# The recurrence's level product with X over both heads of a pair: 128 rows, with Z as two blocks on a diagonal, and M V in one buffer

## What is computed

```python
def step(S, inp):
    r_t, w_t, k_t, v_t, a_t, b_t = inp
    sa = jnp.einsum('bhij,bhj->bhi', S, a_t)
    S = S * w_t[:, :, None, :] + sa[..., None] * b_t[:, :, None, :] + v_t[..., None] * k_t[:, :, None, :]
    return S, jnp.einsum('bhij,bhj->bhi', S, r_t)
```

## Time and profile before

| | |
|---|---|
| median of three runs | 1658.82 us |
| the profiled execution's own time | 1659.36 us |
| its span, first to last instruction | 1657.6 us |
| TensorE busy with products / loading weights | 1457.2 us (88%) / 890.2 us (54%) |
| VectorE, ScalarE, GpSimd busy | 635.0, 365.4, 205.5 us |
| the recurrence within the span | 453.6 to 650.9 us: 197.3 us |

### The profile page before, as it was taken

One profiled execution on the slowest core, in us unless ns is written; L12 is line 12 of the kernel. 1 busy time (PEld: TensorE's weight loads), 2 busy tenths in 40 slices (PEclk: granted clock), 3 DMA queues, 4 the chain that ended last, 5 costly groups with the idle time before them and its releaser, 6 DMA issues. The chain is left out here.

```text
span 1657.6 us, 27544 instructions
## 1 busy us (share of the span) xinstructions
PE 1457.2 (88%) x10747; PEld 890.2 (54%) x10748; DVE 635.0 (38%) x1062; ACT 365.4 (22%) x788; POOL 205.5 (12%) x263
## 2 busy tenths in 40 slices
PE   6999999957778898999929999994996599999968
PEld 4566666645578886444414444442795344444423
DVE  1122453079245452776461111114795311111127
ACT  1233110066423332111101111111232011111111
POOL 4000000000133322110001101104000110110040
PEclk9999999987789999999959999996697699999989
DMA  6573110041110002110259788785105778786453
GB/s 189 134 290 121 26 26 26 0 113 27 30 26 4 5 4 71 56 39 26 111 169 314 267 303 289 254 282 181 62 1 186 269 246 314 257 281 227 159 209 124
DMA packets 137060, 236.96 MB, mean 143 GB/s; under 512 B 20178, under 2 KB 100115, under 8 KB 136682
## 3 DMA queue, kind: packets, MB, share of 16 engines
q1 hardware_dynamic: 113458, 151.01, 28.7%
q0 software_dynamic: 16880, 60.41, 9.9%
q10 hardware_dynamic: 6624, 24.12, 3.6%
HBM read 178.84 MB, written 58.21 MB: 143 GB/s over the span
## 5 line engine op out<-in xcount | busy, mean ns | idle before, releaser
L2257 PE MATMUL ex_pb<-ew_w_gate_up,ex_xT 128*128 x736 | 329.8, 601 | 6.0 <-DVE ex_xT L2302 2.3
L298 PE MATMUL pj_pb<-pj_xT,pj_w 128*128 128x348 f32 (+3 forms) x960 | 282.1, 455 | 0.8 <-ACT pj_xT L322 0.8
L298 PEld LDWEIGHTS pj_pb<-pj_xT,pj_w 128*128 128x128 f32 (+1 forms) x960 | 178.8, 186 | 101.9 <-ACT pj_xT L322 0.8
L2257 PEld LDWEIGHTS ex_pb<-ew_w_gate_up,ex_xT 128*128 128x128 f32 x736 | 138.0, 193 | 165.0 <-issue 164.0
L2240 PE MATMUL ex_pb<-ew_w_down,ex_hiddenT 128*128 x368 | 165.7, 593 | 3.4 <-ACT ex_hiddenT L2327 3.4
L2450 DVE TENSOR_TENSOR ex_hidden<-ex_hidden,ex_pb 128x256 f32<-128x256 f32 x46 | 19.4, 421 | 324.4 <-ACT ex_hidden L2322 324.4
L2240 PEld LDWEIGHTS ex_pb<-ew_w_down,ex_hiddenT 128*128 128x128 f32 x368 | 66.3, 190 | 69.9 <-issue 69.9
L2445 DVE COPY ex_y_rows<-ex_pb 128x512 f32<-128x512 f32 x46 | 31.8, 692 | 134.5 <-PE ex_pb L2240 134.5
L430 DVE SCALAR_TENSOR_TENSOR mixed<-pj_pb,v_mu,mixed 128x347 f32<-128x347 f32 (+3 forms) x42 | 24.0, 572 | 145.7 <-ACT mixed L372 145.6
L2322 ACT ACTIVATE ex_hidden<-ex_pb 128x256 f32<-128x256 f32 x46 | 17.7, 384 | 261.3 <-PE ex_pb L2257 261.3
L1888 PE MATMUL mo_pb<-late_rows,projected_qkv 128*128 128x512 f32 (+1 forms) x144 | 66.6, 608 | 0.0
(11 more groups left out here) (414 smaller groups left out, 2031.4 us busy)
## 6 DMA issues: line engine op xcount, KB each, us to landing
ew_w_gate_up<-in_w_ex_gate SPq DMA_DIRECT2D x32, 1024.0 KB, 8.2
ew_w_gate_up<-in_w_ex_up SPq DMA_DIRECT2D x32, 1024.0 KB, 10.9
ew_w_down<-in_w_ex_down SPq DMA_DIRECT2D x32, 1024.0 KB, 12.9
scratch_slots_out<-ex_y_rows ACTq DMA_DIRECT2D x46, 512.0 KB, 4.8
scratch_slots_out<-pj_tmp POOLq DMA_DIRECT2D x4, 4096.0 KB, 16.7
scratch_x_stored<-x_rows SPq DMA_DIRECT2D x16, 512.0 KB
pj_w<-in_w_in SPq DMA_DIRECT2D x7, 1024.0 KB, 8.9
minus_kk_then_y<-in_x_prompt SPq DMA_DIRECT2D x8, 512.0 KB, 6.0
```

The lines of the kernel that those rows point to most:

```text
L298: last = nc.tensor.matmul(product(at)[:, 0:tn], w[:, s % NW, k, c0:c0 + mrows], xT[:, k, x0:x0 + tn], start=(k == 0), stop=(k == KD - 1))
L2257: last = mm(pb[:, 2 + u, :], xT[:, u, k, :], w[:, k, :], start=(k == 0), stop=(k == KD - 1))
```

## The change

In `level_x` the two products of a pair's heads become one over all 128 rows. X of both heads is read as it lies; Z is kept as a 128x64 matrix with the first head's 64x32 block at the upper left, the second's at the lower right and zeros elsewhere. The zeros come from the mask: the level constants grow from 64x32 (stacked twice) to 128x64 with two blocks on the diagonal, and `take_z` writes each column of Z twice, under the two halves of the mask, 128x512 elements in place of 128x256. The product goes to columns 256 to 511 of bank 6 in place of banks 6 and 7, and `take_x` on VectorE adds both heads in one instruction of 128x256. `MV` becomes one buffer; ScalarE's copy into it waits until both chunks of the step before have been added (`asc`).

```diff
-        Z = m.sb("Z", [P, 2, 4, HALF])
+        Z = m.sb("Z", [P, 2, 4, 2, HALF])
-        MV = m.sb("MV", [P, 2, DA])
+        MV = m.sb("MV", [P, DA])
@@ take_mv
                 act.wait_ge(q["mv"], n + 1)
-                nc.scalar.copy(MV[:, n % 2, :], pb[:, 3, :]).then_inc(q["mvc"], 1)
+                if n:
+                    act.wait_ge(q["asc"], 2 * n)
+                nc.scalar.copy(MV[:, :], pb[:, 3, :]).then_inc(q["mvc"], 1)
@@ level_x
                 for t in range(4):
-                    for par in range(2):
-                        for ch in range(2):
-                            last = mm(pb[fr(ch), 6 + par, P * t:P * t + HALF], X[fr(par), ch, t, :], Z[fr(par), ch, t, :],
-                                      start=True, stop=True)
+                    for ch in range(2):
+                        last = mm(pb[fr(ch), 6, 256 + CH * t:256 + CH * t + CH], X[:, ch, t, :],
+                                  Z[:, ch, t, :, :].rearrange("p a b -> p (a b)"), start=True, stop=True)
@@ take_z
-                tt(flat(Z[:, :, :, :]), columns(6, 0, HALF), eight(f"lev{lev + 1}T"), ALU.mult).then_inc(q["zc"], 1)
+                both = columns(6, 0, HALF).unsqueeze(2).to_broadcast([P, 8, 2, HALF])
+                of_head = const[f"lev{lev + 1}T"][:, :].rearrange("p (a b) -> p a b", a=2)
+                tt(Z[:, :, :, :, :].rearrange("p c t a b -> p (c t) a b"), both,
+                   of_head.unsqueeze(1).to_broadcast([P, 8, 2, HALF]), ALU.mult).then_inc(q["zc"], 1)
@@ take_x on VectorE
-                for par in range(2):
-                    new = halves_of(XT[:, n % 2, :, par, :], lev, 1)
-                    out = pb[:, 6 + par, :].rearrange("p (t s) -> p t s", t=4)[:, :, 0:HALF]
-                    last = tt(new, new, out.rearrange("p t (g b) -> p t g b", b=2 << lev), ALU.add)
-                last.then_inc(q["xe"], 1)
+                new = halves_of(XT[:, n % 2, :, :, :].rearrange("p t a s -> p (t a) s"), lev, 1)
+                out = pb[:, 6, 256:512].rearrange("p (h g b) -> p h g b", h=HA, b=2 << lev)
+                tt(new, new, out, ALU.add).then_inc(q["xe"], 1)
@@ constants
+    tabs.update({k: np.kron(np.eye(2), chunk[k]) for k in LEVELS})
-            mix_const.update({k: sb(layer0, f"k_{k}", [P, CH // 2]) for k in LEVELS})
+            mix_const.update({k: sb(layer0, f"k_{k}", [P, CH]) for k in LEVELS})
```

More of the change, by code:

```diff
@@ L937, in rwkv_chunks @@
         SD = m.sb("ST_decayed", [P, 4, HD])
-        So = MV[0:HD, 0, :].rearrange("p (h j) -> p h j", h=HA)
+        So = MV[0:HD, :].rearrange("p (h j) -> p h j", h=HA)
         pb = m.psum("pb", [P, 8, 512])
@@ L1390, in take_a_by_state @@
                 product = pb[rr, 0:2, :].rearrange("p a (t s) -> p a t s", t=4)[:, :, :, CH:P]
-                tt(by_par(MVAS[rr, :]), product, by_par(MV[rr, n % 2, :]), ALU.add).then_inc(q["asc"], 1)
+                tt(by_par(MVAS[rr, :]), product, by_par(MV[rr, :]), ALU.add).then_inc(q["asc"], 1)
             def take_state(n, ch):
```

## The result

The changed kernel takes 1647.59 us (median of 4 runs, 1640.19 to 1650.47), the kernel before 1661.05 beside it (4 runs, 1653.52 to 1667.32): a ratio of 0.9923, with an interval of 0.9896 to 0.995. It is faster by 0.8%, where 1650 was forecast. The profiled execution took 1647.76 us with a span of 1645.9, 11.7 us less than the span before.

The account below looks back on a forecast made before the run. TensorE bounds the stage, in part through its number of instructions, fetched in blocks of about 256. 1659.4 + 5.9 - 13.4 - 1.2 - 0.6 gave 1650 us; own range 1643 to 1656, with rivals 1642 to 1664.

Parts of the forecast that it names:

- Item 1: `level_x` on TensorE: 16 products of 128*64 last as long as 32 of 64*64; 0, at most 2.8 us.
- Item 2: Changes of TensorE's array form around `level_x` on levels 0, 2, 3: six more a step, +5.9 us (4.6 to 9.0).
- Item 3: TensorE's instruction fetch: 160 fewer instructions a step shorten stalls at edges of 256-instruction blocks, -13.4 us (-9.3 to -19.4).
- Item 4: Half-clock spells after TensorE's long stalls: one of two gone, -1.2 us (0 to -2.5).
- Item 5: Longer `take_z` on VectorE, +0.26 us a level, hidden by ScalarE's copy of X: 0 (up to 10.4 us).
- Item 6: One VectorE addition for two in `take_x` saves 0.06 us once or twice a step: -0.6 us (0 to -2.4).
- V: Theory of the follow-ups: VectorE's one addition for two is the gain; two additions again would cost 8 us or more.
- Items 7 and 8: Wait before ScalarE's copy into one `MV` never ends last, 0; larger masks and moved buffers, 0 (at most 1 us).
- Rival 1: TensorE's stalls go with time, or shrink only with the block count (0 to -2.1 us): 1664 us, chance 0.17.
- rival 2: VectorE bounds a level through the longer `take_z` before `level_x`: 1664 to 1673 us, chance 0.09.
- Rival 3: All TensorE's fetch stalls and both half-clock spells vanish, changes of form cost 0.11 us: 1641.5 us, chance 0.12.

Follow-up runs that it names:

- 320 split: Kernel after, 64-column products of `b_k_by_r`, `b_k_by_a` and `a_by_b` cut into two of 32, 320 instructions a step more: 1686.62 us, ratio 1.0163.
- two merged ones: Kernel after with `b_k_by_a` merged: 1650.30 us; kernel after with 128-row product on levels 1, 4 only, `b_k_by_a` and `b_k_by_r` merged: 1663.36 us.

## Why the prediction was right

**Item 1, the product, 0.** Right. L1191 begins at 526.70, VectorE starts on its result at 527.43: 0.73 us, as before.

**Item 2, changes of form, +5.9.** Right in size, as far as an estimate tells. The overlap fell from 0.18 and 0.21 to 0.07 and 0.08, 0.10 to 0.14 a change. I summed the median distances from group to group over a step, which leaves stalls out: 20.07 us of work before, 20.93 after, so +0.86 a step for 0.78 forecast, +6.0 over seven steps. The second number is borne out by the steps of 20.88 us that hold no stall; for the first no step is free of stalls, and with the lowest distances in place of the medians the difference is 1.0 a step. The Trainium skill, page "TensorEngine Tiling (Array Packing)", section "Tiling Modes", says that changing the tiling mode drains the engine. The trace agrees in so far as the overlap shrinks, by this 0.1 us; 0.07 us of it stay.

**Item 3, fewer instructions, -13.4.** The mechanism was right and the size too small; this is the term that was mis-sized. I let the dense stretches keep stalls: 0.5 us lost for each of 16, and took 11.5 us for six steps. Measured: six steps before are 141.04 - 6 x 20.07 = 20.6 us above their work, after 127.02 - 6 x 20.93 = 1.4 us. So 19.2 us went, the half clock of item 4 in it, against 11.5 + 1.2 forecast. The step that failed is the floor of a block. I took 3.73 us from one pair of stalls as what a block needs, set one stretch of 3.38 us of work against it, and so kept 0.35 us of stall for each dense stretch. But 3.73 is no floor: in the kernel after, the packets of the instruction queue start 3.3 to 5.3 us apart. What holds is a mean, 4.00 to 4.15 us, wherever blocks are late. After the change the mean work of a block (6 x 20.93 / 31 = 4.05 us) is just that, and nearly all blocks are there in time, dense stretches too. That a dense stretch is no longer late because the one before it was not late either is argued from this; no run isolates it. In the other direction I scaled six steps by 7/6, though the first step of the stage is another case: it starts at half clock, lasted 20.1 us before, and became 0.8 us longer. So of the stage's 13.8 us the six steps gave 14.0 (19.2 less some 5.2 of item 2), the rest of it took 0.2 back.

**Item 4, half clock, -1.2.** Mis-sized as well: both spells are gone, not one of two. The only stall over half a microsecond left, 0.83 us before L1211, is followed by full clock:

```profile
551.63:555.43 3.80, 3.48 (x83) 3.09 (x83) 2.06 (x4) 1.16 (x2) 3.01 (x3) 1.00 0.02 4
```

By the bound of item 4 that is up to -2.5; it is part of the 19.2 us and was not measured apart.

**Item 5, `take_z`, 0.** Right, and shown alone within some 4 us: 1.0003 with the wide operation. The cover was ScalarE's copy, as said, with 0.05 us left of it in the row of level 4, and `output` besides. The one wait for `take_z`, 0.7 us in the first step, took the place of one of 0.6 for the copy.

**Item 6, `take_x`, -0.6.** Not contradicted: two additions in the kernel after took 1646.35 - 1645.72 = 0.6 us more. The intervals of these two ratios overlap nearly wholly and reach 0.3% to each side, so the agreement to the tenth is luck; the run excludes the 8 us of V, no more.

**Items 7 and 8, `MV` and constants, 0.** The first shown with item 5. Of the second, 2.0 us lie ahead of the stage, in stages that are the same in both kernels. That is within what one kernel does from one execution to the next: in the second profile of the kernel after, the stage's first step begins 3.0 us later than in the first (465.0 for 462.0 us). Whether the place of buffers and constants adds anything is not shown.

**The rivals.** Rival 1 (1664) fell with 1.2 us of idle by "issue" and 31 packets; rival 2 (1664 to 1673) with the run of the wide `take_z`. Rival 3 (1641.5), that the fetch gives all, had the mechanism nearer than the forecast: nearly all stalls and both spells of half clock went. That the time came out within 2.4 us of the forecast is in part luck. Over the six steps the forecast was -12.7 + 4.7 = -8.0 us and the profiles have -14.0; the factor 7/6 would have had the first step gain where it lost 0.8, and 2.0 us were lost ahead of the stage; and one kernel's executions are up to 10 us apart (1640.19 to 1650.47), more than the miss.

The Trainium skill, page "Runtime: NRT & Kernel Launch", section "Instruction fetch mechanics", says that the fetch is hidden, because the sequencer dispatches more slowly than the memory fills. The runs disagree: 35 blocks take 140 to 143 us with work between some 20 and 22 us a step, each stall ends 2.2 to 3.1 us after a packet's start, and only 30 or 29 blocks leave no idle time. What sets these times, and when the next packet is asked for, is open; the instruction queue's own packets fill only 1.6 to 1.8% of the 16 DMA engines' time.

## What to carry to other kernels

Where small products make TensorE idle by "issue", count the instructions between the stalls, and look for the packets of the instruction queue: if each stall ends at the same distance from a packet's start, the engine waits for instructions. If blocks of about 256 go through at one pace, compare it with the mean work of a block over the whole loop, not of its densest stretch. While the work of a block is shorter than the pace, every instruction removed pays with time in which the engine stood still; once it is longer, only array time counts, and there a merged product can cost more than the several that it replaces. So remove instructions until work and fetch meet, in the form that costs the array least, and stop.

## What the runs showed of the hardware

- A 64*64 product costs nearly the same whether 32 or 64 columns pass: 128 instructions of 32 columns take 2.07 us (16 ns each), 64 of 64 columns 1.16 (18 ns each). `level_x` before and after last 0.62 to 0.67 and 0.69 us for 32 products with 32 columns and 16 with 64, in the two forms.
- Products of 64*128, with alternating row halves as sources, take 1.95 us for 32, 61 ns each. The 64 products of 64*64 that they replace take 1.16 us, four at a time at 18 ns each. No overlap of the wide form shows here.
- Increments of a semaphore on TensorE between products lengthened a group of 32 products from 0.67 to 1.43 us.
- In these kernels a stall for instructions ends 2.2 to 3.1 us after the start of the latest 16 KB packet of the instruction queue (78 spells in ten profiles).
- The first step's time goes with the clock at the stage's beginning. Without increments it took 19.6 to 21.7 us at a mean granted clock of 0.81 to 0.86, 23.1 at 0.72, 24.0 at 0.76, 29.6 at 0.67 and 27.8 at 0.63. Nothing here says what decides how soon the full clock is granted.
- The length of a stall alone does not decide the clock behind it. Two stalls of 1.7 us in the kernel before were followed by 0.56 and 0.55, one of 1.7 us with 128 rows on levels 1 and 4 by full clock (the row below), one of 1.1 us with 320 split by 0.62. In the kernel after (both profiles), with two additions and in the two merged ones, whose stalls are 0.9 us at most, the six steps had full clock throughout.

```profile
573.42:577.22 3.80, 3.80 (x82) 3.36 (x82) 1.36 (x4) 1.56 (x3) 2.83 (x3) 1.00 0.01 4
```
